# A transformer layer on eight cores: the key/value stage moved to the front, fed by half tiles, and the memory projection moved behind attention

## What is computed

```python
q = apply_axial_rope(rms_norm(q.reshape(B, S, N_Q_HEADS, HEAD_DIM), q_norm[l]), cos, sin)
k = apply_axial_rope(rms_norm(k.reshape(B, S, N_KV_HEADS, HEAD_DIM), k_norm[l]), cos, sin)
y_attn = self_attention(q, k, v) @ w_attn_o[l]
y_gmlp = chunked_gmlp(jax.nn.gelu(zg), sgu_norm[l], w_spatial[l], b_spatial[l]) @ w_gmlp_o[l]
y_mem = memory_attention(qm, mem_n, w_mem_kv[l], mq_norm[l], mk_norm[l]) @ w_mem_o[l]
merged = g_a * y_attn + g_g * y_gmlp + g_m * y_mem
x = x + merged @ w_out[l]
x = x + jnp.square(jax.nn.relu(h2 @ w_ffn_up[l])) @ w_ffn_down[l]
```

## Time and profile before

| | us |
|---|---|
| median of 3 runs | 3106.39 |
| lowest, highest | 2795.32, 3147.75 |
| the profiled execution | 2794.46 |
| its span (first to last instruction of the slowest core) | 2792.9 |
| spans of the eight cores | 2763.6 to 2792.9 |

### The profile page before, as it was taken

One profiled execution on the slowest core, in us unless ns is written; L12 is line 12 of the kernel. 1 busy time (PEld: TensorE's weight loads), 2 busy tenths in 40 slices (PEclk: granted clock), 3 DMA queues, 4 the chain that ended last, 5 costly groups with the idle time before them and its releaser, 6 DMA issues.

```text
span 2792.9 us, 33461 instructions; the slowest of 8 cores (2763.6 to 2792.9 us)
## 1 busy us (share of the span) xinstructions
PE 2480.2 (89%) x11427; PEld 1072.0 (38%) x11656; DVE 1224.9 (44%) x1921; ACT 966.2 (35%) x1247; POOL 39.9 (1%) x79
## 2 busy tenths in 40 slices
PE   1798883689999999676999999889999999999998
PEld 0344441323333333222444444333444444444444
DVE  1355555678888888575222222124111211121111
ACT  0456552379999999335111111111101100100100
POOL 0000000000000000000000000000000000000000
PEclk9899996999999999898999999998999999999999
DMA  9456756030000000121334343741434343434342
GB/s 210 94 118 124 141 117 147 16 61 1 1 1 1 1 1 1 24 60 38 76 76 80 71 86 65 181 88 34 91 61 91 61 91 65 87 68 84 72 110 91
DMA packets 29782, 201.32 MB, mean 72 GB/s; under 512 B 2352, under 2 KB 10672, under 8 KB 19504
## 3 DMA queue, kind: packets, MB, share of 16 engines
q0 software_dynamic: 10800, 157.46, 29.0%
q1 hardware_dynamic: 18816, 41.71, 4.6%
HBM read 348.22 MB, written 8.39 MB: 128 GB/s over the span
## 4 chain that ended last, share of the span: by engine, by line
PE 75%; DVE 12%; ACT 5%; issue 4%; DMA 3%; DVEq 0%; ACTq 0%; SPq 0%
PE psum L287 73%; DVE arena L304 7%; ACT arena L301 4%; DVE arena L325 2%; DMA arena<-memT 2%; DMA arena<-xT_own 2%; DVE arena L321 1%; DVE arena L328 1%; PE psum L685 1%; ACT L301 1%; PE psum L291 1%; DVEq L156 0%; PE psum L487 0%; DVE arena L312 0%; DMA arena<-sin_q 0%
## 5 line engine op out<-in xcount | busy, mean ns | idle before, releaser
L287 PE MATMUL psum<-arena 128*128 128x512 bf16 (+1 forms) x10555 | 2417.0, 383 | 212.8 <-ACT arena L301 123.4
L287 PEld LDWEIGHTS psum<-arena 128*128 128x128 bf16 x10784 | 1041.5, 101 | 1557.5 <-issue 447.0
L301 ACT ACTIVATE arena<-psum 128x1024 bf16<-128x1024 f32 (+3 forms) x822 | 677.5, 857 | 1241.8 <-PE psum L287 1215.1
L304 DVE TENSOR_TENSOR arena<-arena 128x512 f32<-128x512 f32 (+5 forms) x1070 | 733.2, 692 | 470.4 <-ACT arena L301 374.7
L304 DVE TENSOR_TENSOR arena<-arena,psum 128x512 f32<-128x512 f32 x304 | 208.9, 688 | 800.5 <-PE psum L287 754.1
L301 ACT ACTIVATE arena<-arena 128x512 f32<-128x512 f32 (+7 forms) x252 | 201.2, 823 | 307.5 <-DVE arena L328 85.1
L325 DVE RECIPROCAL arena<-arena 128x4 f32<-128x4 f32 (+4 forms) x99 | 31.4, 318 | 206.2 <-ACT arena L301 202.7
L301 ACT ACTIVATE arena<-psum,arena 128x512 f32<-128x512 f32 (+3 forms) x151 | 65.4, 503 | 80.7 <-PE psum L287 56.0
L325 DVE RECIPROCAL arena<-psum 128x128 f32<-128x128 f32 x96 | 87.6, 936 | 7.3 <-PE psum L287 6.3
L291 PE MATMUL psum<-arena 128*128 128x128 bf16 x232 | 21.3, 230 | 76.8 <-DVE arena L304 76.7
L328 DVE TENSOR_REDUCE arena<-arena 128x4 f32<-128x512 f32 (+2 forms) x76 | 46.6, 613 | 44.1 <-ACT arena L301 40.5
(11 more groups left out here) (23 smaller groups left out, 50.6 us busy)
## 6 DMA issues: line engine op xcount, KB each, us to landing
arena<-xT_all POOLq DMA_DIRECT2D x16, 2048.0 KB, 14.1
arena<-wp POOLq DMA_DIRECT2D x16, 2048.0 KB, 13.1
arena<-wup POOLq DMA_DIRECT2D x16, 2048.0 KB, 12.5
arena<-wdn POOLq DMA_DIRECT2D x16, 2048.0 KB, 12.9
arena<-xT_own SPq DMA_DIRECT2D x4, 2048.0 KB, 15.1
arena<-wout POOLq DMA_DIRECT2D x4, 2048.0 KB, 12.5
arena<-xT_own SPq DMA_DIRECT2D x8, 1024.0 KB, 22.8
outT<-arena SPq DMA_DIRECT2D x4, 2048.0 KB, 6.3
```

What stands on the lines that cost most here:

```text
L287: P.add("pe", lambda e: e.matmul(out.ap, lhsT=lhsT.ap, rhs=rhs.ap, start=start, stop=stop), reads=[lhsT, rhs], writes=[out])
L301: P.add("act", lambda e: e.activation(out=out.ap, in_=in_.ap, func=func, **kw), reads=rds, writes=[out])
L304: P.add(eng, lambda e: e.tensor_tensor(out=out.ap, in0=in0.ap, in1=in1.ap, op=op), reads=[in0, in1], writes=[out])
```

## The change

- The key/value stage comes first. The start loads gvec, wkv in four quarters (SP) and x in half tiles (POOL, four buffers `xs` of 256 tokens; the first two in quarters). The first four sub-tiles run channel by channel as the quarters come.
- Statistics are spread: `squares(T+1, j)` and `stat_burst(T+1, j)` stand behind sub-tile j of tile T, eight channels of 256 tokens at a time, through two 4 kB buffers `sqs`. `stat_end` is the old end of p1_stats.
- A sub-tile is evacuated by two ACT instructions of 256 columns, keys to `kvK`, values straight to V; p1_C's copy of V goes. Rotary tables: a row part per tile (`trow`) and a constant column part (`tcol`) take the place of cos_k and sin_k; the rotary products are 2 of 512 elements, 4 of 256 and 2 sums per tile. `k_a` shares the place of `k_sq`.
- The order of the tiles differs per core: its own two come last. wq is loaded two channels at a time in tiles 2 to 9 in f32, and scaled into `wq_g` by DVE. Queries are computed from the raw x left in the four halves; the norm of x cancels in the head norm but for epsilon, which is corrected by `epsq`. Scratch is shared with k_pipe. Stage 3 goes.
- `hT` is computed by GpSimd (32 TT and 32 TS of 128 x 512), behind loads of xT_own, recorded ahead of attention.
- Memory queries and the u half alternate in one loop, then comes the memory projection with its loads recorded behind attention (wmkv in the place of KT, memT in that of V), then memory attention, then the v half. `norm_heads` takes the place of qk_pipeline: one square, one reduction, one Sqrt and one RECIP instead of two each, and four products.
- Attention's own instructions stay; `QT`, `attnT`, `pp`, `pt`, `rl` have other places.

```diff
-    xT_all = din("xT_all", [16, 128, 16, 512])
+    xT_all = din("xT_all", [32, 128, 16, 256])
     xT_own = din("xT_own", [2, 128, 16, 512])
-    cos_k = din("cos_k", [16, 128, 4, 128])
-    sin_k = din("sin_k", [16, 128, 4, 128])
+    trow_d = din("trow", [16, 128, 2, 4, 64])
+    tcol_d = din("tcol", [128, 2, 64])
...
+    QT = B(108, [8, 1024], BF16)
+    attnT = QT
...
+    def norm_heads(src, gain, scr, out):
+        hs_ = [slice(0, 2), slice(2, 4)]
+        g4 = lambda ap: ap.rearrange("p (h d) -> p h d", d=128)
+        sq, qn = scr["sq"].all(), scr["qn"].all()
         ss, sd, rs = scr["ss"].all(), scr["sd"].all(), scr["rs"].all()
...
+        big = lambda ref, i: ref.v(lambda ap: g4(ap)[:, hs_[i], :])
+        sm = lambda ref, i: ref.v(lambda ap: ap[:, hs_[i]])
+        ACT(sq, src, AF.Square)
+        RSUM(ss, sq.v(g4))
+        ACT(sd, ss, AF.Sqrt, scale=1.0 / 128.0, bias=eps_col)
+        RECIP(rs, sd)
+        for i in range(2):
+            TT(big(qn, i), big(src, i), sm(rs, i).v(lambda ap: bc(ap.unsqueeze(2), [128, 2, 128])), ALU.mult)
+        for i in range(2):
+            TT(big(out, i), big(qn, i), gain.v(lambda ap: bc(ap.unsqueeze(1), [128, 2, 128])), ALU.mult)
...
+    k_a = k_sq
+    sqs = [B(32, [8, 256], BF16), B(36, [8, 256], BF16)]
+    krope = [B(40, [4, 256], BF16), B(42, [4, 256], BF16)]
...
+    xs = [B(140 + 8 * i, [16, 256], BF16) for i in range(4)]
+    wq_g = B(172, [16, 1024], BF16)
+    wkv_f = [B(172 + 8 * i, [4, 512], F32) for i in range(4)]
...
+    sp_dma(gvec.all(), gvec_d, "c_gvec")
+    for q in range(4):
+        sp_dma(wkv_f[q].all(), wkv_d[:, 4 * q:4 * q + 4, :], f"w_kv{q}")
+        pool_dma(xs[0][4 * q:4 * q + 4], xT_all[0][:, 4 * q:4 * q + 4, :], f"xi0{q}")
+    for q in range(4):
+        pool_dma(xs[1][4 * q:4 * q + 4], xT_all[1][:, 4 * q:4 * q + 4, :], f"xi1{q}")
+    sp_dma(tcol.all(), tcol_d, "c_tcol")
+    sp_dma(grow.all(), grow_d, "c_grow")
+    def x_load(H):
+        pool_dma(xs[H % 4].all(), xT_all[H], f"xs{H % 4}")
+    def t_load(T):
+        sp_dma(trow[T % 2].all(), trow_d[T], f"tr{T % 2}")
+    x_load(2)
+    x_load(3)
...
+    def squares(T, j):
+        src = xs[(2 * T + j // 2) % 4][8 * (j % 2):8 * (j % 2) + 8]
+        dst = sqs[j % 2].all()
+        if j < 3:
+            ACT(dst, src, AF.Square)
+        else:
+            TT(dst, src, src, ALU.mult)
+    def stat_burst(T, j):
+        o = 256 * (j // 2)
+        for k in range(8):
+            c = 8 * (j % 2) + k
+            jj = c % 4
+            P.add("pe", (lambda k, jj, c: lambda e: e.matmul(banks[0][32 * jj:32 * jj + 32, o:o + 256],
+                                                             lhsT=ones.all().ap[:, 0:32], rhs=sqs[j % 2][k].ap,
+                                                             start=(c < 4), stop=(c >= 12),
+                                                             tile_position=(0, 32 * jj)))(k, jj, c),
+                  reads=[ones.all(), sqs[j % 2][k]], writes=[PS(0)])
...
+            o = T - (NT - 2)
+            ACT(epsq[o].all(), t4, AF.Copy, scale=EPS / D, bias=EPS * EPS)
+            MM(PS(1), w32m.all(), sd_bc.all(), True, True)
+            ACT(r_bc[o].all(), PS(1), AF.Sqrt, scale=1.0 / D, bias=eps_col)
+            RECIP(r_bc[o].all(), r_bc[o].all())
...
+    def kv_mm(T, sub):
+        H = (2 * T + sub // 2) % 4
+        o = (sub % 2) * 128
+        for c in range(16):
+            MM(PS(KVB[sub]), xs[H][c, o:o + 128], wkv_g[c], c == 0, c == 15)
+    def kv_evac(T, sub):
+        r = rtok[T % 2][sub:sub + 1]
+        pb = PS(KVB[sub])
+        ACT(kvK[T % 2][sub], pb.v(lambda ap: ap[:, 0:256]), AF.Copy, scale=r)
+        ACT(V[T * 4 + sub], pb.v(lambda ap: ap[:, 256:512]), AF.Copy, scale=r)
...
-    p1_load(0)
-    p1_tabs(0)
-    p1_squares(0)
-    for T in range(NT1 + 1):
-        if T + 1 < NT1:
-            p1_load(T + 1)
-        if T < NT1:
-            p1_stats(T)
+    for hh in range(2):
+        if hh == 1:
+            squares(0, 0)
+            squares(0, 1)
+        for c in range(16):
+            for sub in (2 * hh, 2 * hh + 1):
+                MM(PS(KVB[sub]), xs[hh][c, (sub % 2) * 128:(sub % 2) * 128 + 128], wkv_g[c], c == 0, c == 15)
+        if hh == 1:
+            for j in range(2):
+                stat_burst(0, j)
+            for j in range(2, 4):
+                squares(0, j)
+                stat_burst(0, j)
+    stat_end(0)
+    for T in range(NT):
         if T >= 1:
-            p1_C(T - 1)
-        if T + 1 < NT1:
-            p1_tabs(T + 1)
-            p1_squares(T + 1)
-        if T < NT1:
-            p1_B(T)
+            k_pipe(T - 1)
+        if T + 1 < NT:
+            t_load(T + 1)
+        if 2 <= T < 10:
+            for c in (2 * (T - 2), 2 * (T - 2) + 1):
+                sp_dma(wq_f[c % 2].all(), wq_d[:, c:c + 1, :], f"wqf{c % 2}")
+        for sub in range(4):
+            if T > 0:
+                kv_mm(T, sub)
+            kv_evac(T, sub)
+            if sub % 2 == 1:
+                H = 2 * T + sub // 2 + 4
+                if H < 2 * NT:
+                    x_load(H)
+            if T + 1 < NT:
+                squares(T + 1, sub)
+                stat_burst(T + 1, sub)
+        if 2 <= T < 10:
+            for c in (2 * (T - 2), 2 * (T - 2) + 1):
+                TS(wq_g[c], wq_f[c % 2][0], g_mix(c), ALU.mult)
+        if T == 10:
+            sp_dma(tq[0].all(), cos_q, "tqc")
+            sp_dma(tq[1].all(), sin_q, "tqs")
+            for blk, src_blk in ((0, 1), (1, 0), (2, 3), (3, 2)):
+                COPY(gsw[blk * 32:(blk + 1) * 32], g_q.v(lambda ap: ap[:, src_blk * 32:(src_blk + 1) * 32]), eng="act")
+        if T == 11:
+            TT(tq[0].all(), tq[0].all(), g_q.v(lambda ap: bc(ap.unsqueeze(1), [128, 8, 128])), ALU.mult)
+            TT(tq[1].all(), tq[1].all(), gsw.all().v(lambda ap: bc(ap.unsqueeze(1), [128, 8, 128])), ALU.mult)
         if T >= 1:
...
+            k_tr(T - 1)
+        if T + 1 < NT:
+            stat_end(T + 1)
...
+        bias = epsq[tt // 4][tt % 4:tt % 4 + 1]
+        pq = [PS(KVB[2 * b + i]) for i in R2]
+        for i in R2:
+            ACT(hsl(sq, i), pq[i], AF.Square)
+        for i in R2:
...
+    k_pipe(NT - 1)
+    for tt in range(9):
+        if tt < 8:
+            q_mm(tt)
+        if tt == 0:
+            k_tr(NT - 1)
+        if tt >= 1:
+            q_tr(tt - 1)
+        if tt < 8:
+            q_pipe(tt)
...
+    wqm = B(140, [16, 512], BF16)
+    wzu = B(156, [16, 512], BF16)
+    pool_dma(wqm.all(), wqm_d, "w_qm")
+    pool_dma(wzu.all(), wzu_d, "w_zu")
+    pool_dma(wsT.all(), wsT_d, "c_wsT")
+    sp_dma(sgu.all(), sgu_d, "c_sgu")
+    sp_dma(bsp.all(), bsp_d, "c_bsp")
+    xo = B(124, [4, 512], F32)
+    for t in range(2):
+        for q in range(4):
+            sp_dma(xo.all(), xT_own[t][:, 4 * q:4 * q + 4, :], "xo")
+            for c in range(4):
+                TT(xo[c], xo[c], r_bc[t].all(), ALU.mult, eng="pool")
+            for c in range(4):
+                TS(hT[4 * q + c, t * 512:(t + 1) * 512], xo[c], g_mix(4 * q + c), ALU.mult, eng="pool")
...
+    pt = [B(132 + i, [512], BF16) for i in range(4)]
+    rl = B(136, [512], F32)
...
+    wmkv = B(44, [16, 1024], BF16)
+    memT = B(76, [16, 256], F32)
+    uT = B(92, [4, 1024], F32)
+    memn = B(172, [16, 256], BF16)
+    msq = B(180, [16, 256], BF16)
+    pool_dma(wmkv.all(), wmkv_d, "w_mkv")
+    sp_dma(memT.all(), memT_d, "x_mem")
...
-    for tt in range(9):
-        if tt < 8:
-            p3_mm(tt)
-        if tt >= 1:
-            p3_post(tt - 1)
+    def zu(i):
+        j, t = i // 2, i % 2
+        pb = i % 2
+        for c in range(16):
+            MM(PS(pb), wzu[c, j * 128:(j + 1) * 128], hT[c, t * 512:(t + 1) * 512], c == 0, c == 15)
+        gelu(uT[j, t * 512:(t + 1) * 512], PS(pb), i)
+    for tt in range(8):
+        p3_mm(tt)
+        p3_post(tt)
+        zu(tt)
+        p3_tr(tt)
+    wzv = B(140, [16, 512], BF16)
+    pool_dma(wzv.all(), wzv_d, "w_zv")
+    mrs = B(132, [256], F32)
+    mrs2 = B(133, [256], F32)
+    for c4 in range(4):
+        ACT(msq[4 * c4:4 * c4 + 4], memT[4 * c4:4 * c4 + 4], AF.Square)
+    for c in range(16):
+        MM(PS(0, 256), ones.all(), msq[c], c == 0, c == 15)
+    ACT(mrs.all(), PS(0, 256), AF.Sqrt, scale=1.0 / D, bias=eps_col)
+    RECIP(mrs2.all(), mrs.all())
+    for c in range(16):
+        STT(memn[c], memT[c], g_mem(c), mrs2.all(), ALU.mult, ALU.mult)
+    for mt in range(2):
+        for half in range(2):
+            for c in range(16):
+                MM(PS(1 + half), memn[c, mt * 128:(mt + 1) * 128], wmkv[c, half * 512:(half + 1) * 512], c == 0, c == 15)
+        norm_heads(PS(1), g_mk, m3, qmn[0].all())
+        for h in range(4):
+            TR(Ref(PS(3, 1024, BF16).ap[:, h * 128:(h + 1) * 128], PS(3).gran), qmn[0][h * 128:(h + 1) * 128])
+        COPY(kmT[:, mt * 128:(mt + 1) * 128],
+             PS(3, 512, BF16).v(lambda ap: ap.rearrange("p (h m) -> p h m", m=128)))
+        COPY(vm[mt], PS(2), eng="act")
...
```

(3 more changed lines are left out.)

361 lines of the change are left out of this document (120 added, 241 removed).

## The result

The changed kernel took 2904.5 us in its profiled execution, where the kernel before took 2794.5; the ratio of the two, measured side by side, is 1.040 (95% interval 1.037 to 1.043). It is slower, 74 us above the 2831 forecast and 4.5 us above the range; the prediction had given "slower by over 2%" a chance of 0.42.

The account below looks back on a forecast made before the run. TensorE was taken as nearly the bound in key/value tiles, with 2042 us of attention and tail fixed. Terms -45 + 106 - 65 + 15 + 25 = +36; 2792.9 + 36 + 1.6 = 2830.5, say 2831 us; range 2770 to 2900.

Parts of the forecast that it names:

- the clock term of the tiles: Key/value tiles: TensorE 60% busy with 3 us idle pieces, a tenth of the matmuls at half rate, 1.4 us a tile.
- The start: Front of the kernel: with fewer loads, tile 1 starts its matmuls near 70 us instead of 115.3; -45, between -58 and -35.
- the fourth rival: Start: wkv starves beside the GpSimd queue as memT did and lands after 51.5 us; 10 us more, 2841; chance 0.07.
- The tiles: Key/value tiles: pitch 28.0 us, 407 against 301.1 us for tiles 1 to 15; +106, from +85 to +180.
- three meetings: Key/value tile: TensorE waits three times for ScalarE's evacuations and square, 2.9 us each, the first 0.5 longer; 9.2 a tile.
- The rival with half the matmuls at 1.2 GHz: Key/value tiles: low clock in the gaps makes a tile 33.5 us, +77 more, 2908 us; chance 0.15.
- Loads costed at nothing: Key/value tiles: half-size loads, SP loads and wq scalings cost nothing; without cover each under 2 us a tile.
- Own tokens and queries: Stage before attention: own statistics vanish, k_pipe of tile 15 and queries stay; 96 us against 79.4 + 81.4; -65.
- 8 tiles at 10.2: Query stage: eight query tiles at 10.2 us each, plus 0.2 each for the shared buffer; 83 us.
- hT on GpSimd: Beside attention: GpSimd's 64 operations hold up VectorE, which has little slack; +15, ends 0 and 40.
- The third rival: Attention: GpSimd holds VectorE, +40 instead of +15, and hand-overs slower; 2856 to 2875 us; chance 0.20.
- Behind attention: Memory branch after attention: queries alternating with zu products, projection, memory attention; 150 us against 124.4; +25, ends +15 and +40.

Follow-up runs that it names:

- the filled gaps: The changed kernel with ten unused 128x512 matmuls behind each of the first three sub-tiles of tiles 1 to 14; ratio 1.025, 2871.3 us at the lowest.
- the first experiment: The changed kernel with the square of tile T+1 ahead of the evacuations of sub-tile T; ratio 1.004 to the kernel before, 2809.8 us at the lowest.

## Why the prediction was wrong in size

Three sizes failed, and one wait was missing: the clock term of the tiles (1.4 us a tile in the sum, 3.0 measured), the query tile (10.4 in the sum, 13.5 measured, through waits that the sum did not have), and GpSimd (15 in the sum, 31 measured). Stage by stage:

*The start* (-45 forecast, -58.9). wkv was taken to end at 43 us, by the rate; the rate was right (207 GB/s for 199) but not the order. wkv's quarters landed in 14.4 us at the median and VectorE scaled the last one from 24.4 us on; it is the later halves of x that fill the time to 56 us at 171 GB/s, beside the work. The work behind the last quarter took 32 us (24.4 to 56.4) where the sum had 26, so two errors partly cancel. Nothing starved: the fourth rival is out.

*The tiles* (+106, +134.9). The mechanism and its price stood exactly: three meetings, 2.88 us for 2.9, 26.9 for 26.6 at full clock; the first experiment takes two of the three away, and their time with them. The term that failed is the clock: 1.4 us a tile, "matmuls of 13.8 us, a tenth of them at half rate", where the pitch had 3.0 above 26.9, 2.4 of them the clock by the filled gaps; and 17.2 instead of 15 for tile 15. The clock itself was forecast rightly, 0.8 to 0.9 for a measured 0.89. The step that failed is the one from this clock to time: TensorE busy 20 us a tile (281.9 over 14) at 0.89 loses 2.2, as an estimate, and the sum charged a tenth on the 64 matmuls alone. The rival with half the matmuls at 1.2 GHz, 6.9 a tile, was further off. "Loads costed at nothing" held for the time and not for its reason, "nothing waits behind them": VectorE waited for wq in the changed kernel too (23.4 us in 5 waits), but TensorE never stood longer than 3.9 us for it or anything else. The long pitch hid it, and it was the next bound as soon as that was repaired.

*Own tokens and queries* (-65, -36.7). k_pipe to the first transposes took 13.8 us (492.4 to 506.2), for 13. The step that failed is "8 tiles at 10.2" with 0.2 each for the shared buffer: 13.5 was measured. The cost is in how `q_pipe` names its slices, which the helper's definition shows and the operation count does not; with exact slices the pitch is 10.1, the 10.2 of the prediction.

*hT on GpSimd* (+15, +30.9). The mechanism was named and the ends (0 and 40) held it. The value supposed that the slack and eight pp buffers absorb about two thirds of the 44 us; they don't, for VectorE is busy 485.4 of 552.7 us and 87 instead of 107 sums in 150 us is a backlog that ends in TensorE: it lost 31 us, and the stage nearly as much. Leaving GpSimd out gives 27.3 back. The third rival (+40) was the nearer. The Trainium skill (SBUF — State Buffer, Who interferes with whom) says that it is VectorE instructions with two SBUF inputs that contend with GpSimd's reads; the trace agrees, 970 against 686 ns there and 688 with one input in PSUM. The Trainium skill calls the port pair that the two engines share an exclusive lock there. The trace agrees with this too: all 23 sums that began inside a GpSimd product of two tiles stood until 0.14 us before its end. The figure of 4.5 us that the prediction took from the Trainium skill (GPSIMD Engine Reference, Performance versus the Vector engine) stands there for an addition of two tensors, and a quarter of it 64 times is 72 us and not 65; GpSimd was busy for 118.6 us, its waits for VectorE included.

*Behind attention* (+25, +36.6). The memory projection (31.2 for 31) and memory attention (38.6 for 37.9) are as forecast. The memory queries and u half took 84.1 for 78, as their period is 9.6 to 11.5 and not 9.5, and the v half 7.1 more than the 49.5 of the earlier trace rows, of which the prediction had 3, at a clock of 0.71, for 0.88; why that clock is lower was not tried.

*Sum.* Forecast +36, measured +110.1. Of the 74 missing, 29 are in the tiles, 28 in the queries' slices, 16 in GpSimd, 12 behind attention and 3 in the tail (not explained), less 14 at the start. These 14 came against the forecast, and it is luck that they brought the total as near to the range as 4.5 us. Four of the five terms were given ends, and three of these had the longer end on the costly side; the queries, which missed by 28, had none. The range of the sum followed too little of this.

## What to carry to other kernels

Spreading a burst of work over a loop is only good if the piece that is spread is recorded ahead of what waits for this loop's own results: on an in-order queue, one line decides whether ScalarE squares under 16 matmuls or TensorE stands 2.9 us, three times a tile. Gaps of that size on TensorE are to be priced twice, once as gaps and once as matmuls at the lower clock behind them (here 2.4 us a tile for 9.0). And look at how a helper names a slice before costing its instructions: a view of the whole buffer made two short chains of waits where the data had none.

## What the runs showed of the hardware

- More work on TensorE made the stage shorter: 420 idle matmuls in its gaps, clock 0.89 to 0.99, 33 us less. The gaps were then 0.7 to 1 us instead of 2.9.
- A VectorE sum of two SBUF tiles and a GpSimd product of two tiles, 128x512 f32 each, took turns: all 23 sums that met one ended 0.55 us behind it. Beside the busy VectorE GpSimd took 1674 ns for such a product and 2066 for one by a scalar, where VectorE took 684 for a sum of two tiles.
- A VectorE cast from SBUF to SBUF, with one input only, went from 453 to 612 ns in the mean beside them, up to 1133.
- A switch of ScalarE's table took 1.28 us, and the next operation began at its end (1233.66 to 1234.96 us).
